# SBUF placement of the weight slabs against the activations, and FFN tiles as three 256-column products

## Time and profile before

| | |
|---|---|
| median of three timed executions | 1360.66 us |
| span of the profiled execution | 1358.1 us |
| TensorE busy | 1348.0 us, 99% of the span |
| VectorE, ScalarE busy | 890.4 us, 651.7 us |
| granted TensorE clock, mean | 0.999 |
| FFN stage, gate and up (613.3 to 1101.5 us) | 488.2 us |
| down panels (1101.5 to 1348.3 us) | 246.8 us |

### The profile page before, as it was taken

The page is one execution under the profiler, slowest core; times in us unless marked ns, Lnnn a source line. Parts: engine busy times, 40 slices in busy tenths (PEclk is TensorE's granted clock), DMA queues, the critical chain, the costliest instruction groups (busy, mean ns, idle before and its releaser), DMA issues.

```text
span 1358.1 us, 25677 instructions
## 1 busy us (share of the span) xinstructions
PE 1348.0 (99%) x9644; PEld 1213.2 (89%) x9644; DVE 890.4 (66%) x1320; ACT 651.7 (48%) x910; POOL 23.0 (2%) x50
## 2 busy tenths in 40 slices
PE   9999999999999999999999999999999999999998
PEld 8999999999999998878888888888888888888897
DVE  6787868677785766578666666666666655545545
ACT  5556556474656444355444444444444453334332
POOL 0022000000000000000000000000000000000000
PEclk9999999999999999999999999999999999999999
DMA  8656544445465776644656555555555665556563
GB/s 282 202 190 182 163 150 155 156 145 167 141 183 184 242 228 199 230 173 136 195 184 196 186 187 192 191 187 190 191 189 186 208 231 192 189 171 201 170 204 106
DMA packets 79773, 253.19 MB, mean 186 GB/s; under 512 B 16544, under 2 KB 17504, under 8 KB 79584
## 3 DMA queue, kind: packets, MB, share of 16 engines
q1 hardware_dynamic: 78304, 251.69, 56.5%
q0 software_dynamic: 1408, 0.63, 0.2%
HBM read 248.08 MB, written 2.10 MB: 184 GB/s over the span
## 4 chain that ended last, share of the span: by engine, by line
PE 98%; DVE 1%; ACT 1%; DMA 0%; issue 0%; SPq 0%; DVEq 0%
PE ps L890 23%; PE ps L893 12%; PE ps L879 11%; PE ps L880 10%; PE ps L881 10%; PE ps L902 9%; PE ps L904 9%; PE ps L903 9%; PE ps L1098 1%; PE ps L1117 1%; PE ps L1094 1%; DMA xrow<-x 0%; PE ps L1029 0%; PE ps L1070 0%; PE ps L1043 0%; PE ps L1051 0%
## 5 line engine op out<-in xcount | busy, mean ns | idle before, releaser
L464 DVE TENSOR_TENSOR wlo<-raw,whi 128x1024 fp32r<-128x1024 f32 x450 | 546.6, 1223 | 287.1 <-ACT whi L508 286.0
L508 ACT ACTIVATE whi<-raw 128x1024 fp32r<-128x1024 f32 x450 | 475.1, 1057 | 406.6 <-PE ps L904 184.8
L890 PE MATMUL ps<-hT,whi 128*128 128x512 f32 x1376 | 477.1, 390 | 0.0
L893 PE MATMUL ps<-hT,wlo 128*128 128x256 f32 x1376 | 388.0, 282 | 0.0
L890 PEld LDWEIGHTS ps<-hT,whi 128*128 128x128 f32 x1376 | 258.3, 188 | 54.1
L893 PEld LDWEIGHTS ps<-hT,wlo 128*128 128x128 f32 x1376 | 260.1, 189 | 0.0
L879 PE MATMUL ps<-xT,whi 128*128 128x256 f32 x784 | 224.1, 286 | 0.6 <-DVE wlo L464 0.6
L880 PE MATMUL ps<-xT,whi 128*128 128x256 f32 x784 | 219.0, 279 | 0.0
L881 PE MATMUL ps<-xT,wlo 128*128 128x256 f32 x784 | 218.6, 279 | 0.0
L879 PEld LDWEIGHTS ps<-xT,whi 128*128 128x128 f32 x784 | 147.4, 188 | 1.9 <-issue 1.1
L880 PEld LDWEIGHTS ps<-xT,whi 128*128 128x128 f32 x784 | 147.5, 188 | 0.2
(11 more groups left out here) (271 smaller groups left out, 1407.0 us busy)
## 6 DMA issues: line engine op xcount, KB each, us to landing
raw<-slabs SPq DMA_DIRECT2D x450, 512.0 KB, 3.8
xrow<-x SPq DMA_DIRECT2D x4, 512.0 KB, 6.8
rows<-x SPq DMA_DIRECT2D x4, 512.0 KB, 6.7
gb<-ln_rows SPq DMA_DIRECT2D x4, 512.0 KB, 7.9
eraw<-slabs SPq DMA_DIRECT2D x4, 512.0 KB, 7.0
gb<-ln_rows SPq DMA_DIRECT2D x1, 2048.0 KB, 8.3
out<-rows SPq DMA_DIRECT2D x8, 256.0 KB, 2.4
yb<-u SPq DMA_DIRECT2D x32, 24.0 KB, 3.1
```

Source lines behind the costliest of these rows:

```text
L464: unit.tensor_tensor(wlo[:, s, :], raw[:, s, :], whi[:, s, :].bitcast(F32), ALU.subtract).then_inc(done, 1 + empty_after)
L508: nc.scalar.activation(whi[:, s, :], raw[:, s, :], ACT.Copy).then_inc(hi_ready, 1 + empty + first)
L890: mm(ps[:, bank, :], hi, src[:, kt].rearrange("p a t -> p (a t)"), start=(first and n == 0), stop=False)
L893: ins = mm(ps[:, bank, TOK:512], lo, src[:, kt, 0, :], start=False, stop=done)
```

## The change

- The constants: `FOLD_AT = 112`, `MOVE_UP = 16`, and `ROW_SHIFT` becomes 256 - 112 - 16 = 128.
- A helper `moved_up` places a tile 16 bytes above an allocation. `whi`, `wlo`, `ehi`, `elo`, `mixT` and `act` are placed by it. `a0` is moved so that `xT` lies 112 above `whi` modulo 256.
- `feature_tile` goes. The gate and up tiles are `fold_tile`s: three matmuls of 256 columns into columns 0 to 255 of the bank.
- `tile_sum` goes. ScalarE's Silu reads the gate tile's bank itself, and VectorE's product reads the up tile's bank. TensorE waits for `ffn_silu` before a gate tile and for `ffn_prod` before an up tile, where it waited for `row_free`. ScalarE's Silu waits for the gate tile's last slab.

The new addresses: `whi` 32912 and `wlo` 49296 (144 modulo 512), `xT` 69376, `cT` and `hT` 256 modulo 512, `yT` 0 modulo 512, `mixT` and `act` 400 modulo 512. What moves now lies above what is stationary, modulo 512 (modulo 256), by 112 (112) for `xT`, `cT` and `hT` in `fold_tile`, 368 (112) for `yT`, 256 (0) for `mixT` and `act` in `row_tile`, and 400 (144) for the values.

```diff
-ROW_SHIFT = 192
+FOLD_AT, MOVE_UP = 112, 16
+ROW_SHIFT = 256 - FOLD_AT - MOVE_UP
...
+        def moved_up(name, off, shape):
+
+            room = at(name, off, [P, MOVE_UP // 4 + math.prod(shape)], F32R)[:, MOVE_UP // 4:]
+            axes = " ".join("abc"[:len(shape)])
+            return room.rearrange(f"p ({axes}) -> p {axes}", **dict(zip("abc", shape)))
...
-        whi = at("whi", o, [P, RING, SLAB], F32R); o += RING * SLAB * 4
-        wlo = at("wlo", o, [P, RING, SLAB], F32R); o += RING * SLAB * 4
+        whi_at = o
+        whi = moved_up("whi", o, [RING, SLAB]); o += RING * SLAB * 4
+        wlo = moved_up("wlo", o, [RING, SLAB]); o += RING * SLAB * 4 + 2 * MOVE_UP
...
-        a0 = o
+        a0 = o + (whi_at + MOVE_UP + FOLD_AT - o) % 256
...
-        mixT = at("mixT", a1 + ROW_SHIFT, [P, KT, 2, TOK], F32R)
+        mixT = moved_up("mixT", a1 + ROW_SHIFT, [KT, 2, TOK])
...
-        act = at("act", a3 + ROW_SHIFT, [P, FT, 2, TOK], F32R)
+        act = moved_up("act", a3 + ROW_SHIFT, [FT, 2, TOK])
...
-                    ac.wait_ge(row_free, i * 4 + 11 + 2 * e)
-                    nc.scalar.activation(tmp[:, 1, :], tmp[:, 0, :], ACT.Silu).then_inc(ffn_silu, 1)
+                    if first and e == 0:
+                        ac.wait_ge(early_used, 1)
+                    else:
+                        ac.wait_ge(slab_used, i * FFN_PER + (FFN0 + 4 * e + 2))
+                    nc.scalar.activation(tmp[:, 1, :], ps[:, 4 if first and e == 1 else 0, 0:TOK], ACT.Silu).then_inc(ffn_silu, 1)
...
-            def feature_tile(bank, s, b, src, kts, first, last, whi=whi, wlo=wlo):
...
-                    ins = feature_tile(e, 2 * e + h, n, hT, (k,), k == 0, k == KT - 1, ehi, elo)
+                    ins = fold_tile(e, 2 * e + h, n, hT, (k,), k == 0, k == KT - 1, ehi, elo)
...
-                        row_bank(i * 4 + (8 + e))
+                        pe.wait_ge((ffn_silu, ffn_prod)[e % 2], i * 2 + e // 2)
...
-                        feature_tile(bank + e % 2, k % RING, 0, hT, range(8 * h, 8 * h + 8), h == 0, h == 1
-                                     ).then_inc(slab_used, 1)
+                        fold_tile(bank + e % 2, k % RING, 0, hT, range(8 * h, 8 * h + 8), h == 0, h == 1
+                                  ).then_inc(slab_used, 1)
...
-                    lows(0, 1)
-                    tile_sum(tmp[:, 0, :], 0, v + 1)
-                    lows(2)
-                    tile_sum(tmp[:, 2, :], 1, v + 3)
+                    lows(0, 1, 2)
+                    if first and e == 0:
+                        ve.wait_ge(early_used, 2)
+                    else:
+                        ve.wait_ge(slab_used, v + 4)
+                    ve.wait_ge(ffn_silu, n + 1)
+                    V.tensor_tensor(tmp[:, 3, :], tmp[:, 1, :], ps[:, 5 if first and e == 1 else 1, 0:TOK], ALU.mult
+                                    ).then_inc(ffn_prod, 1)
                     lows(3)
-                    ve.wait_ge(row_free, i * 4 + (12 + 2 * e))
-                    ve.wait_ge(ffn_silu, n + 1)
-                    V.tensor_tensor(tmp[:, 3, :], tmp[:, 1, :], tmp[:, 2, :], ALU.mult).then_inc(ffn_prod, 1)
```

More of the change, by code:

```diff
@@ L16 @@
+import math
 from contextlib import ExitStack
@@ L196, in build @@
         qr = at("qr", o, [P, 2, TOK]); o += 2048
[L197 to L199 removed]
+        assert o <= a3 + FT * 2 * TOK * 4 and a3 + FT * 2 * TOK * 4 + max(4 * PAIRS, ROW_SHIFT + MOVE_UP) <= nc.sbuf_usable_end
+        early = a3 + FT * TOK * 8 - 3 * EARLY * SLAB * 4 - ROW_SHIFT
         eraw = at("eraw", early, [P, EARLY, SLAB])
[L201 to L202 removed]
+        ehi = moved_up("ehi", early + EARLY * SLAB * 4, [EARLY, SLAB])
+        elo = moved_up("elo", early + 2 * EARLY * SLAB * 4, [EARLY, SLAB])
         lnrow = at("lnrow", a1, [P, D], F32R)
@@ L872, in row_bank, with fold_tile @@
                 pe.wait_ge(row_free, m + 1)
-            def fold_tile(bank, s, b, src, kts, first, last):
+            def fold_tile(bank, s, b, src, kts, first, last, whi=whi, wlo=wlo):
                 for n, kt in enumerate(kts):
@@ L882, in fold_tile @@
                              stop=(last and n == len(kts) - 1))
-                return ins
-            def feature_tile(bank, s, b, src, kts, first, last, whi=whi, wlo=wlo):
[L887 to L893, removed]
                 return ins
@@ L1188, in _, with panel @@
                     glu_tile(i, e)
-            def panel(src, src_ready, n_slabs, slot0, v, low, m):
+            def panel(src, src_ready, n_slabs, slot0, v, low, m, read=()):
                 def part(k, t):
@@ L1202, in part @@
                         row_bank(m + t)
+                        if read:
+                            pe.wait_ge(read[t], FT)
                     ins = row_tile(t, (slot0 + k) % RING, t, src, (2 * k, 2 * k + 1), k == 0, k == n_slabs - 1)
@@ L1273, in _ @@
                     panel(act, act_lo, DOWN_PER, DOWN_PER * p, i * (2 * DOWN_PER) + DOWN0 + DOWN_PER * p, late_low,
-                          i * 4 + (8 + 2 * FT + 2 * p))
-            panel(act, act_lo, DOWN_PER, 2 * DOWN_PER, DOWN0 + 2 * DOWN_PER, late_low, 8 + 2 * FT + 4)
-            v, m = DOWN0 + 3 * DOWN_PER, 8 + 2 * FT + 6
+                          i * 4 + (8 + 2 * p), (ffn_silu, ffn_prod) if p == 0 else ())
+            panel(act, act_lo, DOWN_PER, 2 * DOWN_PER, DOWN0 + 2 * DOWN_PER, late_low, 8 + 4)
+            v, m = DOWN0 + 3 * DOWN_PER, 8 + 6
             def last_part(k, t):
@@ L1321, in _ @@
             offset(0, 2, 3, True)
-            pe.wait_ge(row_free, 2 + 8 + 2 * FT + 7)
+            pe.wait_ge(row_free, 2 + 8 + 7)
             turn_shift(1, 0)
@@ L1863, in ffn_turn @@
             def ffn_turn(i, first):
[L1864 to L1871, removed]
-                    V.tensor_reduce(out_, ps[:, bank, :].rearrange("p (a t) -> p t a", a=2), mybir.AxisListType.X, ALU.add
-                                    ).then_inc(row_free, 1)
                 for e in range(2):
```

2 lines of the change are left out of this document (1 added, 1 removed).

## The result

The changed kernel takes 1385.4 us (median of four, 1384.06 to 1385.76) against 1360.4: slower, ratio 1.0182, 95% interval 1.0167 to 1.0196. The prediction was 1340.0 with 1302 to 1368 around it, so the sign was wrong and the range missed.

A forecast was written before the change was run, and what follows sets the result against it. TensorE's own matmul pace was taken as the bound. The third matmul, priced at the new fold pace, and folds at distance 112 gave -8.4 - 9.1 - 3.2 = -20.7 us, all else 0: 1340.0 us, range 1302 to 1368.

The forecast's parts named there:

- What bounds the kernel: Whole kernel: TensorE busy 1348.0 of 1358.1 us and 98% of the chain, so time is its paces, stage by stage.
- Does placement matter at all: Matmul stretches: the trace says a little; folds from `xT` and `yT` differ by 1.0 ns, at distances 32 and 288.
- Step 1: FFN tiles as three matmuls: 4224 at 116.8 ns make 493.4 us against 488.2, so +5.2 us, called sure.
- fixed 3.8 ns for each matmul: Fold against pair at distance 32: one more matmul costs 3.8 ns in itself, of a fold's 10.2 ns excess.
- Step 2: Folds at distance 112: pace 113.6 ns, giving FFN -8.4, `xT` and `cT` -9.1, `yT` -3.2 us.
- the 6.4 ns: Fold matmuls: the part of the 10.2 ns excess that goes with the columns; half, 3.2 ns, was taken as gained.
- worse end of the bound: Folds at 112: at worst the wide rows' excess of 8.1 ns per 256 columns, pace 118.5 ns.
- the prediction's own formula: All folds: the change is 7824 x p - 909.6 us, p the new fold pace, breaking even at 116.25 ns.
- Step 3: Rows at distance 0: no change, as line 1314 there has 233.3 ns; better end 21.2 and 1.7 us.
- Steps 4 to 6: FFN: `tile_sum` out with PSUM reads, new TensorE waits, and the ring with faster TensorE: 0 us each, all hidden.
- 112 is a worse distance: Rival, folds: the wide rows' excess comes to them, pace 118.5 ns, total 1378 us; 9%.
- Placement does nothing: Rival, FFN stage: only the third matmul's +5.2 us stays, total 1365.9 us; 14%.

The follow-up runs named there:

- e_oldplace: The changed kernel's FFN code (three matmuls of 256 columns, Silu and product from PSUM) at the addresses of before, but for `ehi` and `elo`: 1365.67 us, ratio 1.0037.
- map1: Kernel issuing only matmuls, layer left out: three forms at distances 0 to 496 from start 128, then folds at moved starts; fold 114.3 ns at distance 112.
- e_swap112: The changed kernel with the 16 bytes given to the tokens' tiles, weights, `mixT` and `act` at 128 modulo 256, same fold and row distances: 1332.71 us, ratio 0.9797.
- e_rows0: The kernel before with `ROW_SHIFT` = 224 alone, `mixT` and `act` at distance 0 modulo 256, all tiles at multiples of 32: 1352.59 us, ratio 0.9944.
- the maps: Kernels that only issue matmuls, layer left out, sweeping starts and distances of the operands; 67 fold placements repeat between maps and 18 differ by more than 0.6 ns.
- e_odd192: The changed kernel with weights still at 144 modulo 256, but `xT`, `cT`, `hT`, `yT` 192 above them in place of 112: 1334.14 us, ratio 0.9814.

## Why the prediction was wrong, by its steps

**What bounds the kernel** held: the time is TensorE's pace, and no wait grew.

**Does placement matter at all** was answered too faintly. The 1.0 ns between `xT` and `yT` was read as an effect of the distance, 32 against 288 modulo 512, and it is none: folds repeat every 256 bytes in the map, and folds from `xT` themselves have both paces at one placement. In the kernel before, 72 of them in the first head group pace at (188.87 - 180.62) / 70 = 117.9 ns, where the earlier trace rows has 116.8:

```profile
180.62 0.28 PE L880 MATMUL ps<-xT,whi 128*128 128x256 f32 x1
...
188.87 0.28 PE L881 MATMUL ps<-xT,wlo 128*128 128x256 f32 x1
```

And e_oldplace runs the 528 folds of the earlier trace rows at the same addresses at (81.61 - 19.46) / 527 = 117.9:

```profile
19.46 0.36 PE L891 MATMUL ps<-xT,whi 128*128 128x256 f32 x1 [0.23 <-DVE wlo L473]
...
81.61 0.28 PE L893 MATMUL ps<-xT,wlo 128*128 128x256 f32 x1
```

So distance 32 has two paces, as distance 16 has three. The trace of before held this, and the argument for placement was right by luck. The wide rows' 233.2 to 233.3 at three distances looked like a sign against placement, but two of the distances are equally slow in map1 (233.2 at 32, 233.4 at 224), and only 0 has 226.6. Line 1314 was read as the row for distance 0, and three matmuls there did not show what 384 show.

**Step 1** (+5.2 us for the third matmul in the FFN stage) held nearly: +4.4 there in e_oldplace, 4.7 without the help of `ehi` and `elo`. That the total is +5.2 is in part luck, since the front's folds ran 0.6 us slower in its profiled execution (528 x 1.1 ns). The fixed 3.8 ns for each matmul, by which the prediction split the excess, did not hold.

**Step 2 failed**, and with it the sign. I took half of the 6.4 ns off because 112 is far from 0 modulo 256; measured, 3.2 ns came on top (120.0). Two things were wrong. First, the thought of nearness: the map is jagged from 16 to 16 bytes (113.4, 116.8, 118.2 at 16, 32, 48; 120.0, 114.3, 120.0 at 96, 112, 128) and there is no far side. Second, only the distance was weighed. The diff moves the weights to an odd multiple of 16 (`MOVE_UP`), and that was told in the front and then priced at nothing. From an even start 112 gives 113.4, as e_swap112 measured. That this is near the forecast's 113.6 is luck: half of 6.4 had no reason behind it.

The worse end of the bound was also too near: 8.1 ns per 256 columns, pace 118.5, taken from the wide rows, where 120.0 came. With 120.0 in the prediction's own formula, 7824 x 0.1200 - 909.6 = +29.3 us; measured +25.0, since the front's folds stay at 118.5 and 288 from `cT` at 116.7, several stretches of the head groups had 117.8 already, and the rows gain.

**Step 3** (rows at 0: nothing) was wrong by -2.9 us inside its bounds. With an even start it would have been -8.6 for the wide ones, with +0.8 for the narrow ones (e_rows0).

**Steps 4 to 6** held. Silu from PSUM took 0.37 us, the product 0.42, and they fit under TensorE's tiles:

```profile
1122.59 0.37 ACT L835 ACTIVATE tmp<-ps 128x256 f32<-128x256 f32 x1
...
1127.47 0.42 DVE L1882 TENSOR_TENSOR tmp<-tmp,ps 128x256 f32<-128x256 f32 x1 [0.65 <-PE ps L893]
```

**The rivals.** "112 is a worse distance" came nearest, with 9% and a price of 17.6 us for 25.0, but its reason fails too: 112 is one of the best distances from an even start. "Placement does nothing" is e_oldplace's time to 0.3 us, but not this kernel's.

The cause of the loss is shown down to the placement: with one code, distance 112 from start 144 gives an FFN pace of 120.0, distance 112 from start 128 gives 113.4, and distance 192 from start 144 gives 113.4. What stays open is the mechanism. The paces follow the starts of both operands modulo 256, what ran before a stretch or the moment of its start, and the mix of column counts; the runs do not show which part of the chip makes them. The Trainium skill, SBUF — State Buffer, "Who interferes with whom", gives TensorE two independent read ports and says that it never waits on anyone. It speaks of engines that meet and not of addresses. In the maps nothing but TensorE ran, and folds still paced between 113.3 and 124.0 ns by their placement, so the measurement decides against a reading by which placement can't matter.

## What to carry to other kernels

Where TensorE is the bound and both its operands stream from SBUF, the addresses of the two operands are a tuning knob of some 6% (113.3 to 120.0 ns for the same matmul), to be set by measuring the pair of starts and not by a distance alone: one kernel that only issues matmuls maps hundreds of placements in one run, and the places that held still under repetition had their paces in the full kernel's long stretches too (120.0, 113.4, 226.7), to 0.5 ns but for the rows of e_odd192 (230.0 for 231.1). Read each placement more than once, behind different leads, before a long stage is built on it: distances 16 and 192, good in one map and not in another, gave kernels whose times scattered by 24 and 18 us. And a change of form (two matmuls to three) has to be priced at its own placement: here it cost 4.4 us at one and 15.0 at the other. From start 128 at distance 112 it turns round: with nothing else running the pair takes 353 ns (map1) and three matmuls of 256 take 3 x 114.3 = 343.

## What the runs showed of the hardware that I had not expected

- The pace of float32r matmuls depends on the start addresses of both operands modulo 256, in steps of 16 bytes, with all other engines idle: 113.3 to 120.2 ns for 256 columns, 226.7 to 236.7 for 512. Steps of 4 bytes reach 124.0 and 237.8.
- The same code at the same addresses can settle into one of several paces (113.4, 116.7, 118.7 ns at distance 16; 116.7 and 117.8 at 32; 113.4 and 117.8 at 192) and keep it for 490 us. The executions of one kernel then differ (1344 to 1368 us) with the granted clock at its full 2.4 GHz in all.
- Pairs of 512 and 256 columns reach 344.2 ns at best of the two starts that were swept (start 144, distance 224), while three matmuls of 256 reach 3 x 113.4 = 340.2. So more instructions can be faster, where the placement is right.
